# Residual stream with tokens on partitions, norms tile by tile inside the output projections, and output projections with 512 weight columns moving

## What is computed

```python
def rmsnorm(x, g):
    y = x * lax.rsqrt(jnp.mean(x * x, axis=-1, keepdims=True) + EPS)
    return y * g
def modulate(x, g, shift, scale):
    return rmsnorm(x, g) * (1.0 + scale) + shift

for l in range(2):
    m = silu(cond) @ ada_w[l] + ada_b[l]         # 6 vectors of 1024: one set for context, one for latents
    h = modulate(x, norm_mix[l], m[0], m[1])
    x = x + m[2] * mixer_l(h)                    # ends in an output projection
    h = modulate(x, norm_ffn[l], m[3], m[4])
    a = conv3(h @ w_in)                          # 1024 -> 2 * 2816, depthwise over tokens
    x = x + m[5] * ((silu(a_g) * a_u) @ w_out)   # 2816 -> 1024
y = rmsnorm(x, norm_final)
```

## Time and profile before

| | us |
|---|---|
| median of 3 runs | 2135.35 (2135.06 to 2135.97) |
| profiled execution | 2134.29 |
| its span in the trace | 2132.5 |
| TensorE matmul busy | 2032.9 (95%) |
| VectorE (DVE) busy | 938.5 (44%) |
| GpSimd (POOL) busy | 750.8 (35%) |
| ScalarE (ACT) busy | 652.1 (31%) |
| mean granted TensorE clock | 0.971 of full |

### The profile page before, as it was taken

How to read it: one execution, slowest core, us unless ns; L and a number is a source line. 1 busy time by engine, 2 the same in 40 slices (tenths; PEclk the granted TensorE clock), 3 DMA queues, 4 the chain that set the end, 5 groups by cost and what they waited for, 6 DMA issues and landing times.

```text
span 2132.5 us, 32314 instructions
## 1 busy us (share of the span) xinstructions
PE 2032.9 (95%) x12452; PEld 1796.7 (84%) x12452; DVE 938.5 (44%) x1308; ACT 652.1 (31%) x1280; POOL 750.8 (35%) x472
## 2 busy tenths in 40 slices
PE   4999999999999998999999999998979999999998
PEld 2775987698688858999999999895559999999997
DVE  3402410340241044663454264665632773674473
ACT  5222222213222224332232133425533432232232
POOL 2323233223323324333233323436844333333332
PEclk7999999999999998999999999898989999999998
DMA  7431332222223201442333332220002122222211
...
DMA packets 52264, 189.63 MB, mean 89 GB/s; under 512 B 5824, under 2 KB 7104, under 8 KB 51520
## 3 DMA queue, kind: packets, MB, share of 16 engines
...
...
## 4 chain that ended last, share of the span: by engine, by line
PE 88%; ACT 3%; issue 2%; DVE 2%; POOL 2%; POOLq 1%; DMA 1%; DVEq 0%; SPq 0%; ACTq 0%
PE ps L366 35%; PE ps L405 22%; PE ps L381 16%; PE ps L348 2%; PE ps L582 2%; PE ps L421 2%; PE ps L591 1%; ACT pr L1057 1%; PE ps L577 1%; PE ps L353 1%; DMA first_w<-first_dram 1%; PE ps L439 1%; PE ps L456 1%; POOL pr L1182 1%; POOLq L1128 1%
## 5 line engine op out<-in xcount | busy, mean ns | idle before, releaser
L1102 POOL TENSOR_TENSOR w_l<-raw,w_h 128x1024 fp32r<-128x1024 f32 x232 | 564.5, 2434 | 1166.9 <-ACT w_h L787 1166.5
L366 PE MATMUL ps<-h_h,w_h 128*128 128x320 f32 x1696 | 527.6, 311 | 3.5 <-issue 2.0
L366 PE MATMUL ps<-h_h,w_l 128*128 128x320 f32 x1696 | 524.1, 309 | 0.0
L366 PE MATMUL ps<-h_l,w_h 128*128 128x320 f32 x1696 | 523.9, 309 | 0.0
L787 ACT CAST w_h<-raw 128x1024 fp32r<-128x1024 f32 x232 | 245.5, 1059 | 573.5 <-PE ps L405 316.0
L366 PEld LDWEIGHTS ps<-h_h,w_h 128*128 128x128 f32 x1696 | 318.4, 188 | 16.7 <-issue 15.0
L366 PEld LDWEIGHTS ps<-h_l,w_h 128*128 128x128 f32 x1696 | 318.4, 188 | 0.2 <-issue 0.2
L366 PEld LDWEIGHTS ps<-h_h,w_l 128*128 128x128 f32 x1696 | 318.3, 188 | 0.0
L1262 DVE SCALAR_TENSOR_TENSOR xT<-ps,mods,xT 128x128 f32<-128x128 f32 (+2 forms) x264 | 107.9, 437 | 303.1 <-PE ps L405 303.1
L1417 DVE SCALAR_TENSOR_TENSOR cc<-ca,vec,cc 128x641 f32<-128x641 f32 x88 | 233.2, 2650 | 15.1 <-issue 15.1
L405 PE MATMUL ps<-m_h,w_l 128*128 128x320 f32 x704 | 217.1, 308 | 0.0
(11 more groups left out here) (188 smaller groups left out, 2686.5 us busy)
## 6 DMA issues: line engine op xcount, KB each, us to landing
raw<-stream_dram SPq DMA_DIRECT2D x312, 512.0 KB, 3.7
first_w<-first_dram SPq DMA_DIRECT2D x16, 512.0 KB, 15.9
S<-state_dram ACTq DMA_DIRECT2D x4, 1024.0 KB, 7.1
new_state_dram<-st_out ACTq DMA_DIRECT2D x8, 512.0 KB, 3.8
xT<-x_dram ACTq DMA_DIRECT2D x1, 2560.0 KB, 16.2
...
rope_t<-rope_t_dram ACTq DMA_DIRECT2D x1, 512.0 KB, 3.6
rope_a<-rope_a_dram ACTq DMA_DIRECT2D x1, 512.0 KB, 3.6
```

The lines of the kernel that those rows point to most:

```text
L366: mm = nc.tensor.matmul(ps[:, banks + half, 0:HALF], w, x[:, k, lo_hi(half)], start=(k == 0 and n == 0), stop=(k == KT - 1 and n == 2))
L1102: nc.gpsimd.tensor_tensor(w_l[:, r, :], raw[:, s, :], w_h[:, r, :].bitcast(F32), ALU.subtract).then_inc(raw_used[s], 1)
```

## The change

The residual stream becomes `xt`: a tile has 128 tokens on partitions and 1024 features along the row. In `out_proj` the activations are stationary and 512 weight columns move; a token tile has one bank in each of the two passes. The gate then varies along the row: it is kept as a tile over all partitions, loaded with the bias already in it (`gate_b`, 1 MB for each of four gates), and adaLN blocks for gates are spread over partitions by `gate_turn`, two fp32 matmuls of 512 columns. The residual is a multiplication in PSUM and an addition.

The norm is taken token tile by token tile. In the last projection before a norm the last two chunks of the second pass are done together, so that each tile is finished in turn. ACT squares it with a sum along the row, POOL takes the power -0.5, ACT scales, TensorE transposes (`norm_turn`, into banks 5 to 7, tile t-2 behind tile t), DVE applies scale and shift (`norm_f`), ACT rounds (`norm_hi`), POOL (tiles 0, 1, 3) or DVE (tiles 2, 4) makes the remainder. `first_pair` is split into a part for tiles 0 to 2 and one for 3 and 4, and accordingly the two halves of the token axis everywhere become 384 and 256 tokens. The adaLN blocks are spread otherwise over the phases: two now stand in attention's projections and two in FFN 1, and fewer in the retention and FFN 0. x is loaded in five tiles. The final norm's weights lie over all partitions (`fin_g`), and y is stored by SP in five tiles.

```diff
@@ halves of the token axis @@
-HALF = T // 2
+HALF = 3 * P
+REST = T - HALF
...
-            def first_pair(b, norm, ks=range(KT)):
+            def first_pair(b, n, part, ks):
                 slots = [weights(b, w, 0) for w in range(2)]
+                ts = (0, 1, 2) if part == 0 else (3, 4)
                 for k in ks:
-                    pe.wait_ge(hhi_done, KT * norm + k + 1)
+                    hk = k // 4
+                    pe.wait_ge(hhi_done, HALVES * n + half_at(n, ts[-1], hk) + 1)
                     for w, s in enumerate(slots):
                         for wt in (w_h, w_l):
-                            for half in range(2):
-                                nc.tensor.matmul(ps[:, 2 * w + half, 0:HALF], wt[:, s, k * P:(k + 1) * P],
-                                                 h_h[:, k, lo_hi(half)], start=(k == 0 and wt is w_h), stop=False)
-                    wait_rest(pe, norm, k)
+                            nc.tensor.matmul(ps[:, 2 * w + part, 0:width(part)], wt[:, s, k * P:(k + 1) * P],
+                                             h_h[:, k, lo_hi(part)], start=(k == 0 and wt is w_h), stop=False)
+                    wait_lo(pe, n, ts, hk)
                     for w, s in enumerate(slots):
-                        for half in range(2):
-                            mm = nc.tensor.matmul(ps[:, 2 * w + half, 0:HALF], w_h[:, s, k * P:(k + 1) * P],
-                                                  h_l[:, k, lo_hi(half)], start=False, stop=(k == KT - 1))
-                        if k == KT - 1:
+                        mm = nc.tensor.matmul(ps[:, 2 * w + part, 0:width(part)], w_h[:, s, k * P:(k + 1) * P],
+                                              h_l[:, k, lo_hi(part)], start=False, stop=(k == KT - 1))
+                        if k == KT - 1 and part == 1:
                             mm.then_inc(chunk_done, 1)
+            def norm_turn(n, t, hks=(0, 1)):
+                pe.wait_ge(scaled, TT * n + t + 1)
+                for hk in hks:
+                    x = half_at(n, t, hk)
+                    if x >= 3:
+                        pe.wait_ge(f_done, HALVES * n + x - 2)
+                    for kk in range(4):
+                        mm = nc.tensor.transpose(ps[:, 5 + x % 3, kk * P:(kk + 1) * P],
+                                                 scaled_x[:, t, hk * 512 + kk * P:hk * 512 + (kk + 1) * P], ident)
+                    mm.then_inc(turned, 1)
+            def early_turns(n):
+                return lambda t: norm_turn(n, t - 2) if t >= 2 else None
+            def first_tiles(b, n, o):
+                pe.wait_ge(res_done, 10 * o + 9)
+                first_pair(b, n, 0, range(0, 2))
+                norm_turn(n, 3)
+                first_pair(b, n, 0, range(2, 5))
+                norm_turn(n, 4)
+                first_pair(b, n, 0, range(5, KT))
+                first_pair(b, n, 1, range(KT))
...
-            def out_proj(b, j0, i, tiles, xh, xl, ready, free, last=False):
-                j = j0
+            def out_proj(b, j0, i, tiles, xh, xl, ready, free, last=False, between=None):
+                kcs = tiles // 2
                 for mh in range(2):
-                    for kc in range(tiles // 2):
-                        s = weights(b, j, i)
-                        ready(kc)
-                        for at in range(8):
-                            bank = out_bank(mh, at, last)
-                            mt, half = bank // 2, bank % 2
-                            if kc == 0:
-                                free(mh, bank)
-                            for kk in range(2):
-                                k = 2 * kc + kk
-                                c = kk * 512 + mt * P
-                                wh, wl = w_h[:, s, c:c + P], w_l[:, s, c:c + P]
-                                for n, (w, x) in enumerate(((wh, xh), (wh, xl), (wl, xh))):
-                                    mm = nc.tensor.matmul(ps[:, bank, 0:HALF], w, x[:, k, lo_hi(half)],
-                                                          start=(k == 0 and n == 0),
-                                                          stop=(k == tiles - 1 and n == 2))
-                            if kc == tiles // 2 - 1 and at < 7:
-                                mm.then_inc(out_done, 1)
-                        mm.then_inc(chunk_done, 1)
-                        j += 1
+                    together = [(kc,) for kc in range(kcs)]
+                    if last and mh == 1:
+                        together = together[:-2] + [(kcs - 2, kcs - 1)]
+                    for chunks in together:
+                        slots = []
+                        for kc in chunks:
+                            slots.append(weights(b, j0 + mh * kcs + kc, i))
+                            ready(kc)
+                        for t in range(TT):
+                            bank = out_bank(mh, t, last)
+                            if chunks[0] == 0:
+                                free(mh, t)
+                            for kc, s in zip(chunks, slots):
+                                for kk in range(2):
+                                    k = 2 * kc + kk
+                                    wh, wl = (w[:, s, kk * 512:(kk + 1) * 512] for w in (w_h, w_l))
+                                    for n, (x, w) in enumerate(((xh, wh), (xh, wl), (xl, wh))):
+                                        mm = nc.tensor.matmul(ps[:, bank, :], x[:, k, t * P:(t + 1) * P], w,
+                                                              start=(k == 0 and n == 0),
+                                                              stop=(k == tiles - 1 and n == 2))
+                                if t == TT - 1:
+                                    mm.then_inc(chunk_done, 1)
+                            if chunks[-1] == kcs - 1:
+                                if t < TT - 1:
+                                    mm.then_inc(out_done, 1)
+                                if mh == 1 and between is not None:
+                                    between(t)
...
+            def gate_turn(par, copied):
+                pe.wait_ge(ada_copied, copied)
+                for s in range(2):
+                    mm = nc.tensor.matmul(ps[:, 4 + par + s, :], sel[:, s:s + 1].to_broadcast([P, P]), ada_o[:],
+                                          start=True, stop=True)
+                mm.then_inc(ada_turned, 1)
+            def opening(b):
+                first_pair(b, 0, 0, range(0, 4))
+                ada_first(2)
+                first_pair(b, 0, 1, range(0, 2))
+                ada_turn(0, 3)
+                first_pair(b, 0, 1, range(2, 4))
+                ada_first(3)
+                ada_turn(0, 4)
                 for t in range(TT):
+                    norm_turn(0, t, (1,))
+                first_pair(b, 0, 0, range(4, KT))
+                first_pair(b, 0, 1, range(4, KT))
...
+            def norm_square(n, t, half):
+                if n == 0:
+                    act.wait_ge(x_in[t], 16)
+                    cols, to = slice(0, D), ssum
+                else:
+                    act.wait_ge(res_done, 10 * OUT_OF[n] + 5 * half + t + 1)
+                    cols, to = slice(half * 512, half * 512 + 512), (rest, ssum)[half]
+                nc.scalar.activation(scaled_x[:, t, cols], xt[:, t, cols], ACT.Square,
+                                     accum_out=to[:, t:t + 1]).then_inc(sq_done, 1)
+            def norm_scale(n, t):
+                act.wait_ge(rms_ready, TT * n + t + 1)
+                nc.scalar.activation(scaled_x[:, t, :], xt[:, t, :], ACT.Copy,
+                                     scale=r_rms[:, t:t + 1]).then_inc(scaled, 1)
+            def norm_hi(n, t, hk):
+                act.wait_ge(f_done, HALVES * n + half_at(n, t, hk) + 1)
+                nc.scalar.copy(h_h[:, 4 * hk:4 * hk + 4, half_cols(t)],
+                               scaled_x[:, t, hk * 512:hk * 512 + 512].rearrange("p (k q) -> p k q", k=4)
+                               ).then_inc(hhi_done, 1)
...
+                for j in range(tiles - (0 if n is None else 2)):
                     if b.m0 + j + RING < MAINS:
                         hi(b, j + RING, 0)
+                    if n is not None and j == tiles // 2 - 1:
+                        for t in range(TT):
+                            norm_square(n, t, 0)
+                if n is None:
+                    return
+                for t in range(TT):
+                    norm_square(n, t, 1)
+                    if n == 4:
+                        continue
+                    if t >= 2:
+                        for hk in range(2):
+                            norm_hi(n, t - 2, hk)
+                    norm_scale(n, t)
+                if n == 4:
+                    return
+                for t in (3, 4):
+                    for hk in range(2):
+                        norm_hi(n, t, hk)
+                    hi(b, tiles - 5 + t + RING, 0)
...
+            next_gate(7, 3)
```

(61 more changed lines are left out.)

806 lines of the change are left out of this document (368 added, 438 removed).

## The result

The change saves about half of what was forecast: 2120.1 us (median of 14 runs, 2117.1 to 2131.9), where the kernel before, measured beside it, has 2134.0 (14 runs, 2131.6 to 2137.5). The ratio is 0.9941, interval [0.9927, 0.9956]. The forecast was 2108; the time lies inside the stated range of 2098 to 2124, near its upper end. The runs of the changed kernel lie 15 us apart, those of the kernel before 6.

The account below looks back on a forecast made before the run. TensorE, busy 95% of the span, was taken as the bound, through its matmul times and idle seams. Projections, seams, clock, gates, end and opening summed to -27.7 us from 2134.29, with 1.06 for the median, rounded to 2108; range 2098 to 2124.

Parts of the forecast that it names:

- output projections: Chunks of 30 matmuls of 512 columns (6.80 us) replace 48 of 320 (7.04), over 68 chunks: -16.1 us.
- seam 1 with its clock: Retention to FFN 0: 8.5 us lost instead of 20.7, with 0.8 added for a slowed clock: -11.4 us.
- seam 2 with its clock: FFN 0 to attention: 7.6 us lost instead of 15.0, with 0.8 added for a slowed clock: -6.6 us.
- seam 3 with its clock: Attention to FFN 1: 12.7 us lost instead of 10.6, including a 4.2 us wait for final norm weights, plus clock: +2.9 us.
- gate turns: Eight adaLN blocks spread by two fp32 512-column matmuls (1.72 us) instead of four 2-column ones (0.95): +6.2 us.
- end: After the last matmul, final products and tile stores take 9.5 us instead of 16.2: -6.7 us.
- opening: Kernel start: 1 MB of gate bias loads ahead of weights and half tiles pass DVE: +4 us, bounds -3 and +8.
- no fixed cost is saved: Rival on output projections: overhead comes with columns, not matmuls, so 16.1 us more, 2124; chance 0.04.
- DVE becomes the bound behind projections: Rival: DVE at 1.56 a tile against 1.36 stalls 7 projections inside phases 1.5 us each, 2118; chance 0.08.
- the 2121 of a cost of 2.5 ns: Output projections priced with the Trainium skill's 2.5 ns a matmul, saving 3.1 us: 2121; no separate chance given.
- The wait itself: At each seam TensorE waits about 3.6 us for the rounded first half, DVE setting the pace; bounds 0 and 10.
- halves of 384 and 256 columns: Token halves of 384 and 256 instead of 320 and 320 cost nothing, if a 256-column matmul keeps 120 ns.

Follow-up runs that it names:

- the second profile of the changed kernel: The changed kernel run again with nothing edited, for a profile nearer its usual time: 2124.2 us, span 2124.6.
- two pads: y_h, y_l moved 64 bytes up and m_h, m_l 448, in the changed kernel with early rounding and written-out loop: 2099.8 us, against 2109.3 without.
- early rounding: At each seam the last two weight chunks rounded before tiles 3 and 4, remainders before tile 3's, against the changed kernel: 2118.8 us against 2124.2.
- the two runs with that order changed: VectorE scales tile 2's first half before tile 4's residual: 2113.0 us against 2109.3; with ScalarE's rounding also earlier, two pads added: 2102.9 against 2099.8.
- written-out loop: TensorE's loop over heads 1 to 3 written out: changed kernel 2118.1 us; kernel before 2128.3 against 2134.7.

## Why the prediction was wrong, by its own steps

The sum against the second profile of the changed kernel. A stage is measured between the starts of its first matmul and the next stage's in TensorE's timeline, in both kernels; blocks that only moved (1.93 us, with their turn 2.88) are set off against each other. Seam 1, for one: from the last projection's first matmul to the next free-running tile 67.8 us before and 60.3 after, -7.5, of which -0.7 is the projection and +0.8 the gate turn, so -7.6.

| step | forecast | measured |
|---|---|---|
| output projections | -16.1 | -6.4 |
| seam 1 with its clock | -11.4 | -7.6 |
| seam 2 with its clock | -6.6 | -0.9 |
| seam 3 with its clock | +2.9 | +0.3 |
| gate turns | +6.2 | +6.2 |
| end | -6.7 | -7.5 |
| opening | +4.0 | +5.4 |
| loop boundaries and steps | 0 | +2.1 |
| features of group 2 in FFN 0 | 0 | -0.9 |
| first features of FFN 1 | 0 | +1.5 |
| other features | 0 | -0.2 |
| sum, us | -27.7 | -8.0 |

The spans differ by 2132.5 - 2124.6 = 7.9. This profile's execution, 2126.5 us, lies 6.4 above the median of the changed kernel's runs, and that of the kernel before within 1.1 of its own, which is why the medians differ by 13.9. A stall of the loop and what follows it cost 4.2 us, so 0 to 2 of them explain some 8 of the 15 us between the runs of the changed kernel.

*Output projections: the mis-sized term.* "A chunk was 48 matmuls of 320 columns (7.04 us) and is 30 of 512 (6.80 us)": the price was right for the operand it was read from and was carried to operands that lie elsewhere. The earlier trace rows show 0.2268 for h stationary (d = 0). The fixed cost is 13.4 ns at d = 0, 15.6 at d = 192 and 20.0 at d = 64. 44 FFN chunks at 7.00 and 16 of the retention at 6.87 lose 44 x 0.20 + 16 x 0.07 = 9.9 us, and two pads gave 9.5 of it back. The rows gave no warning: in the kernel before m was the moving operand, at another distance from the weights than h, and both had 0.1467; at 320 columns the place made no difference. Three numbers beside the forecast lie nearer to 2120.1, all by luck: the rivals "no fixed cost is saved" (2124; a part of it is saved) and "DVE becomes the bound behind projections" (2118; no wait came inside a projection), and the 2121 of a cost of 2.5 ns. The Trainium skill, "TensorE: Matmul & The Clock Gate", Back-to-back issue gap, gives these 2.5 ns beside N/2.4 for an isolated matmul and speaks of no addresses; the measured 13.4 to 20.0 ns decide against it for these streams.

*Seams 1 and 2: a wait that was not counted.* "I followed the queues from the start of those chunks, in the order printed above for TensorE and ACT", and POOL was left out. Its order puts the last two w_l behind h_l of tile 3: they end 47.8 and 51.5 us behind the start of the last projection in the profile of the result, 40.6 and 43.0 with the early rounding, so that raw slots came free some 7 to 9 us later than they could. Seam 1 had an adaLN block, which needs four raw chunks, already, and the change had put one into seams 2 and 3. Against the second profile the early rounding gives back 3.0 and 3.7 us of the 3.8 and 5.7 missing there (at seam 1 against other profiles less). Another 1.0 at seam 1 lies in the projection itself, whose first 14 matmuls run at 1.2 GHz behind a wait (granted 0.50 from 795 to 800 us): there one of 512 columns takes 0.427 us, its columns alone, and no fixed cost is saved (3.2 us lost there against 2.1 in the kernel before). What else is missing at seam 2 stays open. The wait itself was right (3.3 against 3.6; by the forecast's own times, 19.3 - 16, it is 3.3), and so were its place in VectorE's queue, by the two runs with that order changed, and the transposes. Of the blocks moved into seams 2 and 3 the forecast says "their 1.9 us move and count for nothing": right in what they take themselves and wrong in what they wait for. The second block of FFN 1 waits for raw too, +1.5.

*Seam 3.* The forecast had TensorE's gate turn 4.2 us late, by a landing of the final weights 9 us behind their issue. They landed 7.2 us behind it, 5.8 with the early rounding; ACT did wait (4.50 us), but TensorE lost nothing by it, and moving it gained nothing. The landing was put too late, and the wait for raw, which the block did have there (0.85 us), was not counted.

*Loop boundaries.* The forecast said nothing on them, and so put them at nothing. The 0.99 us of "issue" in head 2's first row of the kernel before was not looked at, nor that it could grow: that the changed kernel with early rounding and pads comes to 2099.8, below the forecast, is owed to the written-out loop too, for which the forecast had counted nothing.

*Right:* halves of 384 and 256 columns (112.53 us for 768 records against 112.64), gate turns, the end, the opening within 1.4 us; the sign, and that no wait came inside a projection and 256 columns kept their 0.120 us. The 19.7 us between the two sums are thus 9.7 of projections, 9.5 of seams 1 and 2 and 2.1 of the loop, less 2.6 that seam 3 gave by luck (the landing came sooner than forecast), and 1 of the rest; against the median 12 us are missing.
